# First attention of a two-layer kernel in tiles of 8 rows by 16 columns, two heads at a time, probabilities scaled on GpSimd

## What is computed

```python
qx, kx, vx, ux = split_proj(hx @ w_in[i])            # 8 heads of 64; ux feeds the convolution
kvc = hc @ w_in[i][:, ATT_DIM:3 * ATT_DIM]           # keys and values of the 256 context tokens
qx_rot, kx_rot = axial_rope(qx, ...), axial_rope(kx, ...)
# every query sees a window of 8 rows x 16 columns of keys (shifted inwards at the borders) and all context keys
s_win = einsum('bqhd,biqjhd->bhqij', qr_rot, kw) * scale + bias      # bias from rpb[head, row offset, column offset]
s_ctx = einsum('bqhd,bchd->bhqc', qr, k_ctx) * scale
p = softmax(concatenate([s_win, s_ctx]))
out = p_win @ vw + p_ctx @ v_ctx
# conformer_conv: h = a * sigmoid(b); depthwise convolution of 31 taps along the tokens; layer norm; silu
x_new = x + g1 * (concatenate([attn_x, conv_x]) @ w_out[i])
```

## Time and profile before

| | us |
|---|---|
| median of 3 runs | 2840.64 (2840.02 to 2843.12) |
| the profiled execution | 2845.75 |
| its span, first to last instruction | 2843.8 |
| projections, from the first product to the last | 58.6 to 324.9 |
| first attention, first score to the meeting after it | 332.3 to 639.7 |
| layer norm of the convolution and turn back | 639.7 to 672.1 |
| output projection | 672.1 to 759.5 |

### The profile page before, as it was taken

How to read it: one execution, slowest core, us unless ns; L and a number is a source line. 1 busy time by engine, 2 the same in 40 slices (tenths; PEclk the granted TensorE clock), 3 DMA queues, 4 the chain that set the end, 5 groups by cost and what they waited for, 6 DMA issues and landing times.

```text
span 2843.8 us, 34883 instructions
## 1 busy us (share of the span) xinstructions
PE 2695.1 (95%) x14056; PEld 2177.4 (77%) x14056; DVE 1400.0 (49%) x1526; ACT 722.3 (25%) x1004; POOL 941.3 (33%) x443
## 2 busy tenths in 40 slices
PE   6999799998899999999989989999999999989899
PEld 3888577776688888888867757887888878778777
DVE  3635888874454445444447668883003221352331
ACT  4200133333221111111114436662000020141010
POOL 1334522201344443444433310004434434523333
PEclk8999799999899999999999999999999999999999
DMA  5111222212111111111121100001111111112112
GB/s 238 38 38 53 70 77 77 62 65 82 44 38 52 47 49 52 44 52 44 52 89 45 45 16 1 1 1 45 48 63 45 52 45 45 67 38 104 45 38 89
DMA packets 36674, 155.88 MB, mean 55 GB/s; under 512 B 4164, under 2 KB 4296, under 8 KB 35016
## 3 DMA queue, kind: packets, MB, share of 16 engines
q1 hardware_dynamic: 33264, 127.04, 13.1%
q10 hardware_dynamic: 1528, 20.71, 1.8%
q0 software_dynamic: 1760, 6.36, 0.9%
HBM read 145.70 MB, written 8.39 MB: 54 GB/s over the span
## 4 chain that ended last, share of the span: by engine, by line
PE 84%; DVE 10%; issue 2%; DMA 2%; ACT 1%; POOL 1%; DVEq 0%; ACTq 0%; POOLq 0%
PE region L265 22%; PE region L267 22%; PE region L266 22%; PE pv L696 4%; DVE conv L820 3%; PE region L796 2%; PE aux L684 2%; PE aux L1399 2%; PE pv L342 1%; PE region L798 1%; DVE prob L1480 1%; DVE tmp L418 1%; DMA x_sb<-x_t 1%; PE pv L506 1%; DVE h_lo L412 1%
## 5 line engine op out<-in xcount | busy, mean ns | idle before, releaser
L1772 POOL TENSOR_TENSOR w_hi<-w_raw,der 128x1024 fp32r<-128x1024 f32 x186 | 360.1, 1936 | 1662.4 <-PE region L267 1616.7
L265 PE MATMUL region<-h_hi,w_hi 128*128 128x512 f32 x1760 | 694.0, 394 | 43.8 <-DVE h_lo L412 20.6
L266 PE MATMUL region<-h_lo,w_hi 128*128 128x512 f32 x1760 | 690.0, 392 | 0.0
L267 PE MATMUL region<-h_hi,w_lo 128*128 128x512 f32 x1760 | 689.6, 392 | 0.0
L1775 POOL TENSOR_TENSOR w_lo<-w_raw,w_hi 128x1024 fp32r<-128x1024 f32 x186 | 500.0, 2688 | 14.6
L265 PEld LDWEIGHTS region<-h_hi,w_hi 128*128 128x128 f32 x1760 | 333.7, 190 | 123.2 <-issue 48.8
L267 PEld LDWEIGHTS region<-h_hi,w_lo 128*128 128x128 f32 x1760 | 333.4, 189 | 70.0
L266 PEld LDWEIGHTS region<-h_lo,w_hi 128*128 128x128 f32 x1760 | 333.8, 190 | 68.5
L265 PE MATMUL region<-ff_hi,w_hi 128*128 128x512 f32 x512 | 199.2, 389 | 0.0
L266 PE MATMUL region<-ff_lo,w_hi 128*128 128x512 f32 x512 | 199.2, 389 | 0.0
L267 PE MATMUL region<-ff_hi,w_lo 128*128 128x512 f32 x512 | 199.2, 389 | 0.0
(11 more groups left out here) (323 smaller groups left out, 4269.3 us busy)
## 6 DMA issues: line engine op xcount, KB each, us to landing
w_raw<-units SPq DMA_DIRECT2D x186, 512.0 KB, 3.6
w_raw<-w_ada_late SPq DMA_DIRECT2D x32, 512.0 KB, 3.6
ada_buf<-w_ada SPq DMA_DIRECT2D x4, 2048.0 KB, 14.1
toep<-rpb_pad POOLq DMA_DIRECT2D x16, 288.0 KB, 5.6
x_sb<-x_t ACTq DMA_DIRECT2D x2, 2048.0 KB, 14.0
x<-x_t ACTq DMA_DIRECT2D x1, 4096.0 KB, 13.0
x_spill<-x ACTq DMA_DIRECT2D x1, 4096.0 KB, 11.8
x<-x_spill ACTq DMA_DIRECT2D x1, 4096.0 KB, 14.3
```

Source lines behind the costliest of these rows:

```text
L265: pe.matmul(dst, wh, xh, start=first, stop=False)
L266: pe.matmul(dst, wh, xl, start=False, stop=False)
L267: return pe.matmul(dst, wl, xh, start=False, stop=last)
L1772: pool.tensor_tensor(w_hi[:, s], w_raw[:, s], one_col.broadcast_to([P, 1024]), ALU.mult)\
```

## The change

Five parts, all in the first layer:

1. **Tiles.** A tile is 8 grid rows by 16 columns of queries (128), for two heads. Its keys are 12 rows by 32 columns (384, read from `k_rot` through a strided pattern) and the 256 of the context: 640. So there are 32 iterations instead of 64, each with two heads, h = 2j in partitions 0 to 63 and 2j+1 in 64 to 127. The scores of the two heads are written alternately, from the two halves of the array's rows, into the two halves of `region`; the values alternately, with 64 columns of v stationary and the transposed probabilities moving, into partitions 0 to 63 and 64 to 127 of one PSUM bank. The result comes out transposed, so that `o_tok` and the turn back fall away; ACT and DVE write it as `mixa_hi` and `mixa_lo`.
2. **Bias** comes ready made from HBM (24 tiles of 128x2x384, `bias_load` on SP, four buffers); POOL makes none.
3. **Division.** The probabilities are scaled by the reciprocal of their sum before they are transposed, on POOL: 64 tensor_scalar of 128x640 (`na_pool`). `na_prob` has three buffers.
4. **Order of the projections.** u first, then k, v, q; 92 of the 124 taps are done beside them (10 after each pair of u, 4 after each k, 7 after each v, 2 after each q), 32 in the attention, one an iteration. There is no meeting between projections and attention.
5. **v and late modulation.** v goes through HBM (`v_spill`) to get its windows in order (16 DMAs of 64 KB for each pair of heads). The late modulation runs one step in every iteration, into spare columns of `region`; its 32 turned rows are added at the end at once.

```diff
-KEYS = 10 * W_GRID
-NKT = (KEYS + CTX) // P
+Q_ROWS, Q_COLS = 8, 16
+K_ROWS, K_COLS = 12, 32
+WIN = K_ROWS * K_COLS
+KEYS = CTX + WIN
+NKT = KEYS // P
...
-STAGE_UNITS = [("q", 4), ("k", 4), ("v", 4), ("u", 8), ("out1", 8), ("mlp", 16 * FF_GROUPS), ("lat", 6),
+STAGE_UNITS = [("u", 8), ("k", 4), ("v", 4), ("q", 4), ("out1", 8), ("mlp", 16 * FF_GROUPS), ("lat", 6),
...
+    def na_pe(e, pos):
+        def scores(i):
...
+            for s in range(2):
+                wait_region(e, uses[s])
+            late_pe(e, i)
+            if i:
+                late_turn_pe(e, i - 1)
+            for s in range(2):
+                e.matmul(region[:, s, 0:CTX], q_t[rows[s], j, q], k_ctx[rows[s], j], start=True, stop=True)
+            for lo, n in ((0, 8), (8, 4)):
+                for s in range(2):
+                    at = CTX + lo * K_COLS
+                    last = e.matmul(region[:, s, at:at + n * K_COLS].rearrange("p (r c) -> p r c", c=K_COLS),
+                                    q_rot[j][rows[s], q], keys[rows[s], lo:lo + n], start=True, stop=True)
+                    if lo:
+                        last.then_inc(sem("na_scored"), 1)
...
+        def values(i):
+            reach(e, "na_pt_act", 2 * i + 2)
+            reach(e, "na_pt_dve", i + 1)
+            if i:
+                reach(e, "na_lo", i)
...
+            for b in range(NKT):
+                for s in range(2):
+                    d = slice(64 * s, 64 * s + 64)
+                    v = v_ctx[:, b, j * P + 64 * s:j * P + 64 * s + 64] if b < 2 else v_pair[j % 2][:, cb, rb + b - 2, d]
+                    last = e.matmul(pv[d, 0, 0:P], v, na_prob_t[:, i % 2, s, b], start=(b == 0), stop=(b == NKT - 1))
...
+        for i in range(NA_N + 3):
+            if i < NA_N:
+                scores(i)
+            if 2 <= i < NA_N + 2:
+                turn(i - 2)
+            if i >= 3:
+                values(i - 3)
...
+    def na_pool(e):
+        for i in range(NA_N):
+            reach(e, "na_inv", i + 1)
+            for s in range(2):
+                c, p = 2 * (i % 4) + s, na_prob[:, i % 3, s]
+                e.tensor_scalar(p, p, na_inv[:, c:c + 1], None, ALU.mult).then_inc(sem("na_prob"), 1)
...
+    def na_dve(e, pos, ch, taps):
+        def most(i, s):
...
+            e.tensor_tensor_reduce(na_prob[:, i % 3, s], region[:, s, 0:KEYS], bias_t[n % 4][:, s], 1.0, -3.0e38,
+                                   ALU.add, ALU.max, na_max[:, c:c + 1]).then_inc(sem("na_most"), 1)
+            reach(e, "na_most", 2 * i + s + 1)
+            e.tensor_scalar(na_neg[:, c:c + 1], na_max[:, c:c + 1], -1.0, None, ALU.mult).then_inc(sem("na_shift"), 1)
+            if s:
+                e.sem_inc(free[s], 1)
+            else:
+                late_dve(e, i)
+                e.sem_inc(free[s], 1)
...
+        for i in range(NA_N + 4):
+            if i < NA_N:
+                most(i, 0)
+                most(i, 1)
+            if 2 <= i < NA_N + 2:
+                move(i - 2)
+            if i >= 4:
+                lo(i - 4)
+            if 1 <= i < NA_N + 1:
+                norm(i - 1)
+            for n in left[len(left) * i // NA_N:len(left) * (i + 1) // NA_N]:
+                conv_tap(e, ch, n)
```

524 lines of the change are left out of this document (295 added, 229 removed).

## The result

The changed kernel takes 2779.4 us (median of four, 2772.8 to 2781.2) where the kernel before takes 2841.9 in the same runs: a ratio of 0.978, with a 95% interval of 0.9764 to 0.9795. The forecast was 2764 us, with a range of 2742 to 2818. The profiled execution is the fastest of the four, 2772.84 us with a span of 2770.8; the terms of the prediction have to be held against this one. Its distance from the profiled execution before, which was the slowest there, flatters the change: -73.0 us in the table, -62.5 between the medians.

The account below looks back on a forecast made before the run. PE bounds the old attention; the new one is bound by a ring of waits through DVE's low part. Start +2, attention -71, layer norm -8 give -77: 2845.75 to 2769, median 5.1 lower, 2764 us; range 2742 to 2818.

Parts of the forecast that it names:

- The ring: Attention iteration: scores, DVE's maxima through low part, PE's values, late modulation, turn, scores again; 6.7 plus 0.2, 6.9 us.
- Row halves overlap: Attention scores on PE: two heads' products run at once in the array's row halves, 1.28 us instead of 2.4 serial.
- Rival (a): Attention: row halves don't overlap or clock falls part-time; 7.9 us an iteration, 2795; with (d) 0.27, far part 0.08.
- rival (b): Attention: PE's clock stays at 1.2 GHz throughout; iteration 9.8 us, 2854 in all; chance 0.09 together with (c).
- POOL's scaling: Attention, probabilities on POOL: 1.0 us each, bounds 0.7 and 2.6, starting when the tap ends, two of up to 2.3 hidden.
- rival (c): Attention: POOL is the bound; at 4.6 us a scaling the iteration is 9.4 us; chance 0.09 together with (b).
- The start: Projections ahead of attention: DVE, not PE, sets the first maximum, at 338 us against 335.92; +2 us, bounds -6 and +10.
- Rival (d): Projections: POOL's splits delay three DVE operations instead of two, start 32 us later, 2796; with (a) 0.27.
- The loads: SP's loads in the attention, 0.8 MB in 6.9 us, two iterations ahead of use: costed at nothing.
- The loop's sum: First maximum to layer norm: 31 x 6.9 = 214, 6 for lower clock level, 13 for the end; 233 us, -71.
- The layer norm: After the attention: without the turn back, squares follow DVE's deviations by one, at 654.4 instead of 662.8; -8 us.
- All that follows stays.: Output projection and everything after it, including the feed-forward loop, were to stay unchanged: 0 us.

Follow-up runs that it names:

- the first two runs: Changed kernel with DVE's low part taken ahead of the two maxima, 2762.5 us; then the reciprocal that starts POOL's scalings also ahead of them, 2720.2 us.
- the run in one row half: Score products of both heads read the same 64 partitions, against the 2703.3 us kernel with DVE's low part and reciprocal early and SP's loads reordered: 2733.4 us.
- the run with the loads alone in turn: Changed kernel with only SP's loads reordered: late load of iteration 2 ahead of bias and second v_pair, v_pair pieces in four portions; 2769.2 us.
- low part and reciprocal first: Changed kernel with DVE's low part and the reciprocal that starts POOL's scalings both taken ahead of the maxima: 2720.2 us, ratio to before 0.957.
- the run with the low part first: Changed kernel with DVE's low part of pair i-4 taken ahead of the maxima of i, nothing else moved: 2762.5 us.

## Why the prediction was right, and which terms were off

- **The ring.** The step that carried the forecast held: PE's own work (4.65 us, said 4.4) does not set the iteration, the ring through DVE's low part does. 6.9 was said, 6.68 is measured. The parts: DVE 2.80 (said 3.0), values 1.25 (1.25), late modulation 0.57 (0.58), turn 0.31 (0.21), scores 1.36 (1.28). The 0.2 for changes between tilings were not needed. That it is this ring, and not some throughput, the first two runs show: 6.25 and then 4.65 us without any less work.
- **Row halves overlap.** Taken at 1.28, shown by the run in one row half (2.37 against 1.28). Rival (a) had this as one of its two conditions; it falls.
- **The clock.** The other condition of (a), and rival (b), asked whether PE falls to 1.2 GHz (0.50) with its pauses. It did not: 0.95 in the middle, with two iterations of 8.2 us in which it fell. In the changed kernel those cost 3 us together.
- **POOL's scaling.** This term was mis-sized: 1.0 us said, 1.885 alone and 2.84 beside the tap measured, above the upper bound of 2.6. "It starts when the tap ends" misread the order: the reciprocal stands ahead of the tap in DVE's stream, so POOL starts at 451.58, 0.18 us into the tap, and that is where the extra microsecond comes from. "Two of up to 2.3 us each are hidden": the pair of 4.70 was just outside that and was hidden even so. But the reason given, transposes that have 10 us, was wrong, and so was the place from which rival (c) decides. The prediction had POOL's throughput in mind, 4.6 us a scaling; there is a second ring, POOL's pair plus 1.75 us, and the run with doubled scalings shows it at 10.25 us. POOL would have decided from a pair of 4.9 us on, 2.5 a scaling. The scalings stayed hidden with 0.2 us to spare in each iteration, which nothing in the prediction secured: that was luck.
- **The start.** Said +2 and 338, measured -0.5 and 335.4. DVE sets it, as said: PE stands for 16.9 us ahead of its second late modulation (about 15 said). What the taps took from the idle time was read rightly from the earlier trace rows. Rival (d) falls.
- **The loads.** "I cost them at nothing" is the step that failed. The sentence behind it asked for a few us once per pair of heads; it came once, 7.8 us at the start, and the run with the loads alone in turn gives it back (10.2 us between medians, 5.5 between traces). The error was to count bytes (0.8 MB an iteration) instead of the issues ahead of a load on its queue: 16 small ones take 7.7 to 9.0 us on SP.
- **The loop's sum.** 233 said, 236.1 measured: 31 intervals take 215.4 (220 said; 31 of 6.67 would be 207, the wait for the load and the clock make up the rest), the end 20.8 instead of 13. There the four last pairs wait for scalings that nothing hides, at a mean clock of 0.74.
- **The layer norm.** -8 said, -9.8 measured, by the mechanism named: the squares follow the deviations at once. PE's first sums ran warmer besides (7.15 us instead of the 8.83 of the earlier trace rows).
- **"All that follows stays."** It did not: 4.9 us more in the profiled execution, made of 11.1 more in the loop and 6.1 less behind it, of which only the first is the change's. The change shortened PE's stream ahead of the feed-forward loop by some 830 instructions, and the loop came to lie where each jump back stands for 3 us. No rival had this.

The difference of -73.0 beside the -77 of the forecast looks closer than it is. Against the forecast, the load cost 8 us more, the end of the attention 8 and the loop 11, while the rest of the 31 intervals took 12 less, the start 2.5 and the layer norm 2; 6 less came from a part behind the loop that varies by itself. Between medians the change gives -62.5. Of the 15 us by which the forecast missed the median, 4 are the terms, and the rest is that the forecast took the median 5.1 us under the profiled execution, where now it is 6.6 above it. The mechanism of the attention was right; that the total fell so well within the range owes something to errors of opposite sign.

## What to carry to other kernels

In a software pipeline over several engines, write down every ring, with what each engine does in a row between taking and giving, not only the busiest engine; an operation that another engine waits for goes ahead of one that nobody waits for yet. Here two moved lines gave nearly as much (59 us) as the whole change (62.5). Cost a load by the issues that stand ahead of it on its queue as well as by its bytes, and spread small ones. Where a part that was not touched becomes slower, look at the jumps of the program.

## What the runs showed of the hardware

- A loop's jump back on PE costs nothing that shows or 1.9 to 3.5 us depending on where the loop lies in PE's stream. Its body here has some 1,580 instructions. Counted in the program, it stalled with its first instruction at number 7636 and 8660, and did not at 8466 and 7698; modulo 256 these are 212, 212, 18 and 18. The steps of 62 and 194 are in the traces' counts of records; the numbers themselves are not (7580 and 8406 instructions stand ahead of the loop there in the changed kernel and the one before, some records being missing), so the offsets may be off by some tens. Other places were not tried. The Trainium skill, page "Runtime: NRT & Kernel Launch", section Instruction fetch mechanics, says that a taken branch to instructions no longer held has to wait for a fetch, and that the stream comes in blocks of 256. The runs agree with the first: the stalls are at taken branches only. The two shifts came out as blocks of 256 would have it, but that it is an offset in such a block that counts is not shown.
- Instructions that only wait for what is long fulfilled are not free on PE: they stand 0.106 us apart, twice what was expected. 194 at the start of the program take 21 us and put off its first product from 11.4 to 22.7 us; 62 there vanish in PE's wait of 11 us; 62 ahead of the layer norm take 6.7 us, of which 3.4 show behind PE's last products.
- GpSimd takes 1.885 us for 128x640 float32 times a column. A DVE operation with two inputs in SBUF that runs already when it starts adds 0.96 us (all 30 such cases in the changed kernel); one that begins while the scaling runs adds nothing and is not held up itself (26 cases with low part and reciprocal first); maxima with one input in PSUM add nothing.
- Products of two row halves run side by side even where they don't strictly alternate: the six of two heads in a row take 1.82 us, alternating 1.28, in one row half 2.37.
- PE's clock did not follow its busy share or its number of products here: 0.85 busy with 9.2 records of products per us had a granted clock of 0.87, 0.80 busy with 9.8 had 1.00 (both in the run with the low part first), and 0.73 busy with 8.5 had 0.95 (the middle of the changed kernel). The first was in an uneven rhythm. What decides is not shown.
